# A 26-product block algorithm for ten of eleven bodies of each FFN up projection

## The reference

```
def conv_ffn(x, w_in, conv_w, conv_b, w_out):
    h = causal_dwconv(x @ w_in, conv_w, conv_b)
    gate, val = h[..., :D_FF], h[..., D_FF:]
    return (jax.nn.gelu(gate) * val) @ w_out
...
def _conv_ffn(h, w_up, conv_w, conv_b, w_down):
    u = _dwconv(h @ w_up, conv_w, conv_b)
    gate, val = jnp.split(u, 2, axis=-1)
    return (jax.nn.gelu(gate, approximate=True) * val) @ w_down
```

## Time and profile before

| | us |
|---|---|
| median of 3 runs | 3307.51 |
| lowest and highest run | 3304.76 and 3310.20 |
| span of the profiled execution | 3308.8 |
| TensorE busy in it | 3243.1 |
| VectorE, ScalarE, GpSimd busy | 1734.4, 1034.2, 1227.8 |

### The profile page before, as it was taken

The page is one execution under the profiler, slowest core; times in us unless marked ns, Lnnn a source line. Parts: engine busy times, 40 slices in busy tenths (PEclk is TensorE's granted clock), DMA queues, the critical chain, the costliest instruction groups (busy, mean ns, idle before and its releaser), DMA issues.

```text
span 3308.8 us, 51491 instructions
## 1 busy us (share of the span) xinstructions
PE 3243.1 (98%) x16994; PEld 2617.8 (79%) x16994; DVE 1734.4 (52%) x2856; ACT 1034.2 (31%) x2119; POOL 1227.8 (37%) x983
## 2 busy tenths in 40 slices
PE   9999999999999999999999999999999999999998
PEld 7787888867777788886446888878888688788887
DVE  6675446555555545646446555345463544354544
ACT  3533233123333323313326333133221334223312
POOL 4344444323221345442001343444443431544444
PEclk9999999999999999999999999999999999999999
DMA  3223222221111222222211211222222211122222
GB/s 136 77 84 102 78 93 82 77 82 59 58 52 39 77 95 77 82 95 71 70 45 32 58 57 57 83 70 83 95 82 96 71 52 65 52 83 95 83 91 81
DMA packets 68682, 249.53 MB, mean 75 GB/s; under 512 B 7568, under 2 KB 7568, under 8 KB 68544
## 3 DMA queue, kind: packets, MB, share of 16 engines
q1 hardware_dynamic: 68544, 247.72, 22.7%
HBM read 245.59 MB, written 2.10 MB: 75 GB/s over the span
## 4 chain that ended last, share of the span: by engine, by line
PE 91%; DVE 4%; ACT 2%; issue 2%; DMA 0%; DVEq 0%; SPq 0%; ACTq 0%
PE psum L2434 56%; PE psum L545 6%; PE psum L2369 5%; PE psum L2611 4%; PE psum L1964 3%; PE psum L1497 3%; PE psum L1524 2%; PE psum L1989 1%; PE psum L577 1%; PE psum L2623 1%; PE psum L1551 1%; PE psum L615 1%; ACT scratch L1211 1%; PE psum L599 1%; DVE stream L3003 1%
## 5 line engine op out<-in xcount | busy, mean ns | idle before, releaser
L2434 PE MATMUL psum<-scratch 128*128 128x256 f32 (+2 forms) x3600 | 809.5, 381 | 0.3 <-issue 0.2
L2434 PEld LDWEIGHTS psum<-scratch 128*128 128x128 f32 x3600 | 683.6, 190 | 101.4 <-issue 1.9
L3286 POOL TENSOR_TENSOR scratch<-w_ring 128x512 f32<-128x512 f32 (+2 forms) x160 | 201.0, 1256 | 1114.2 <-DMA w_ring<-units 901.4
L2699 ACT ACTIVATE scratch<-psum 128x256 f32<-128x256 f32 (+2 forms) x480 | 184.8, 386 | 852.5 <-PE psum L2434 821.9
L3106 DVE TENSOR_TENSOR scratch<-scratch,psum 128x256 f32<-128x256 f32 (+2 forms) x264 | 107.8, 422 | 485.5 <-PE psum L2434 471.6
L2434 PE MATMUL psum<-scratch,w_ring 128*128 128x256 f32 (+2 forms) x1200 | 274.0, 381 | 0.0
L2434 PEld LDWEIGHTS psum<-scratch,w_ring 128*128 128x128 f32 x1200 | 227.9, 190 | 33.3
L2434 PE MATMUL psum<-acts,w_ring 128*128 128x256 f32 (+2 forms) x1088 | 245.1, 383 | 1.2 <-ACT acts L2115 0.9
L2434 PEld LDWEIGHTS psum<-acts,w_ring 128*128 128x128 f32 x1088 | 207.0, 191 | 32.7 <-ACT acts L2115 1.2
L3293 POOL TENSOR_TENSOR scratch<-w_ring 128x512 f32<-128x512 f32 (+2 forms) x160 | 229.8, 1436 | 0.0
L2784 ACT ACTIVATE scratch<-scratch,params 128x512 f32<-128x512 f32 (+2 forms) x176 | 144.0, 818 | 272.1 <-DVE scratch L3106 272.1
(11 more groups left out here) (495 smaller groups left out, 4981.7 us busy)
## 6 DMA issues: line engine op xcount, KB each, us to landing
w_ring<-units SPq DMA_DIRECT2D x463, 512.0 KB, 3.7
residual<-x_t SPq DMA_DIRECT2D x4, 528.0 KB, 6.0
out_t<-residual SPq DMA_DIRECT2D x2, 512.0 KB, 3.4
out_t<-residual SPq DMA_DIRECT2D x1, 768.0 KB, 4.4
params<-cols SPq DMA_DIRECT2D x1, 568.5 KB, 10.4
out_t<-residual SPq DMA_DIRECT2D x1, 256.0 KB, 3.3
gate_w_sb<-gate_w SPq DMA_DIRECT2D x1, 96.0 KB, 10.1
```

Source lines behind the costliest of these rows:

```text
L2434: mm = nc.tensor.matmul(out, weights(k), moving(k), start=(p in (1, 2, 5) and k == 0), stop=(k == h - 1), skip_group_check=(p != 2))
L2699: nc.scalar.activation(kept(q, n, H), quad_bank(q, p, H, b), ACT.Copy).then_inc(q_copied, 1)
L3286: g.tensor_tensor(s(1), row(1, 0), row(1, 1), ALU.add).then_inc(q_weight, 1)
```

## The change

The first body of each FFN up projection stays two quads. The ten others treat their 4 units as a whole: weights in 4 x 4 blocks (unit by quarter of the input features), input in 4 x 2 blocks (quarter of the features by half of the tokens). A product is now two matmuls, and a table of 26 products takes the place of the 28 pairs of matmuls of two quads: 52 matmuls a body. The tables also say what each engine does: `RANK_PRODUCTS` names for each product its weight block (under 16 one of the ring, else buffer number plus 16), how many of POOL's sums must be done, its input block, its bank and whether it opens the bank. `RANK_SUMS` lists POOL's 18 instructions of a body, 29 sums of 128x256, eleven instructions making two sums each (128x512 in all), into 16 buffers in `SCR`. `RANK_TERMS` lists to which rows a product is added: 8 first terms are copied by ACT, 18 later ones added or subtracted by DVE. `RANK_MOVING` lists 20 sums of the input, made once an FFN by DVE. The semaphores `r_product`, `r_weight`, `r_first` and `r_later` are the old `x_loaded0` to `x_loaded3`, and `r_moving` is the old `lru_conv`.

`W` gets four more slots, `WX`, at the end of `SCR`, and an FFN's units alternate between the two sets of four. The convolution now runs by half rows (T/2 tokens) in two banks of PSUM: ACT writes the first tap to the bank, DVE adds the two others in place, ACT takes the gelu from there to `A`, and DVE multiplies `A` by the other bank. These steps of body j-1 stand between the terms of body j, at the places in `PIECE_AT`. `xp` exists twice. The mixer's tables move into `SCR`. The sums of the input for the down projection are spread over the last bodies.

```diff
+RANK_PRODUCTS = (
+    (19, 2, ('v', 0, 0), 'turns', True),
+    (22, 4, ('x', 1, 1), 3, True),
+    (13, 0, ('v', 1, 0), 4, True),
+    (24, 5, ('x', 2, 0), 'turns', False),
+    (26, 6, ('v', 2, 0), 3, False),
+    (27, 7, ('v', 5, 0), 4, False),
...
+    (6, 0, ('v', 17, 0), 4, True),
+    (17, 18, ('v', 16, 0), 'turns', False),
+    (15, 0, ('x', 3, 0), 2, True),
+)
+RANK_SUMS = (
+    ('add', ((0, 2, 10), (1, 5, 13),), 0, 0),
+    ('add', ((2, 1, 16), (3, 6, 17),), 1, 0),
+    ('sub', ((4, 8, 9), (5, 10, 11),), 0, 0),
+    ('add', ((6, 19, 20),), 3, 0),
...
+    ('add', ((1, 13, 1),), 0, 0),
+)
+PIECE_AT = (1, 7, 13, 19)
...
+            def rank(n, j, src, H):
...
+                        pe.wait_ge(r_weight, rank_weighed(n, j, sums))
...
+                    for q in range(2):
+                        mm = nc.tensor.matmul(PS[:, bank, 0:H], weights(q), moving(q), start=(opens and q == 0), stop=(q == 1),
+                                              skip_group_check=True)
+                    mm.then_inc(r_product, 1)
...
+            def rank_weights(n, j):
...
+                    for buffer in RANK_SUM_AGAIN[at]:
+                        if j > 1:
+                            pool.wait_ge(r_product, rank_done(n, j - 1, RANK_LAST_USE[buffer] - 1))
...
+                    g.tensor_tensor(blocks([RANK_BUFFERS + o for o, _, _ in sums]), blocks([a for _, a, _ in sums]), blocks([e for _, _, e in sums]),
+                                    ALU.add if op == "add" else ALU.subtract).then_inc(r_weight, 1)
...
+                    nc.scalar.activation(PS[:, 6 + val, 0:H], scratch(2128 * (j % 2), 4, 532)[:, 2 * pair + val, half * H:half * H + H],
+                                         ACT.Identity, bias=PAR[:, w0 + 3:w0 + 4], scale=PAR[:, w0:w0 + 1]).then_inc(shared("tap", name), 1)
...
+                    y = PS[:, 6 + val, 0:H]
+                    v.scalar_tensor_tensor(out=y, in0=xps[j % 2][:, 2 * pair + val, half * H + k:half * H + k + H], scalar=PAR[:, w0 + k:w0 + k + 1],
+                                           in1=y, op0=ALU.mult, op1=ALU.add).then_inc(shared("mid" if k == 1 else "conv", name), 1)
...
-                with pe.Fori(0, NF // 2) as i:
-                    quads(i, BODIES[name], UNITS[name], KD // 2, T, CHUNKS[name], lambda k, t, e: h(k)[:, t:e], ready=normed)
+                quads(0, BODIES[name], UNITS[name], KD // 2, T, CHUNKS[name], src, ready=normed)
+                for j in range(1, RANK_UP + 1):
+                    rank(n, j, src, T // 2)
```

More of the change, by code:

```diff
@@ L102 @@
         CHUNK_LAST.append(_b - 1)
+CHUNK_HALF = [(c + 1) % 2 for c in range(len(CHUNK_LAST))]
+for _name in ("ffn0", "ffn1", "ffn2", "ffn3"):
+    _c = CHUNKS[_name]
+    CHUNK_HALF[_c + 1], CHUNK_HALF[_c + 2], CHUNK_HALF[_c + 3] = CHUNK_HALF[_c], 1 - CHUNK_HALF[_c], CHUNK_HALF[_c]
 class Chain:
@@ L3125, in ffn @@
[L3125 to L3134 removed]
+                        moving(chunk, m, KD // 2, src, H, T)
```

615 lines of the change are left out of this document (488 added, 127 removed).

## The result

The changed kernel takes **3477.39 us** (median of four runs, 3476.34 to 3478.85). The kernel before took 3307.83 us in the runs beside it. The ratio is 1.0513, with a 95% interval of 1.0498 to 1.0527, so the change costs 5.1%. The forecast was 3410 us with a range of 3365 to 3460. The direction was right and the size was 67 us too small: the measured time lies 17 us above the upper end of the range. The profiled execution has a span of 3477.1 us.

The account below looks back on a forecast made before the run. The prediction took TensorE, busy 98% of the span, as the bound now, with POOL's late start adding waits after the change. From 3307.5 us, +68 + 4 + 31 = +103 gave 3410 us, 80% range 3365 to 3460.

Parts of the forecast that it names:

- fewer matmuls and down projection, nothing waits: Up bodies go from 56 to 52 matmuls, saving 70 us if TensorE never waits; down projection adds 4 us.
- gaps behind POOL, bodies 2 to 10: TensorE waits for POOL before the first, second and sixth products: 3.53 to 3.69 us a body.
- clock in those bodies: Clock falls in half of the 36 new bodies, 1.7 us each: +31 us, ends 0 and 61.
- the first of the ten bodies: VectorE enters the body after the two-quad one late, 1 to 3 us, taken as 2; body called even.
- +68: Bodies 2 to 10 in four FFNs: net loss of 1.76 to 1.96 us a body, clock falls not included.
- POOL's place: POOL starts a body's sums only after the previous body's 25th product, since they write buffer 1: 3.53 us wait in ffn0.
- third gap: Before a body's sixth product, TensorE waits 0.25 us for POOL's seventh instruction.
- The expected rows: Profile would show TensorE idle for POOL, some 36 times 2.1 and 1.15 us, and TensorE, not DMA, releasing POOL.
- The rival on the other side: TensorE never waits and the up bodies lose 70 us: 3242 us; chance that it hardly waits 0.06.
- POOL's 1.27 us: POOL's 512-wide sums in the new bodies keep 1.27 us beside VectorE, not 1.73 us.
- clock stays up: Rival: no clock falls in the new bodies, all else as forecast: 3380 us, range 3365 to 3390, chance 0.27.
- Banks behind VectorE and ScalarE: In new bodies both free PSUM banks in time; 0 to 1 us a body if not. POOL-or-banks-late or clock-always-down case: 0.20.

Follow-up runs that it names:

- finer spread: Changed kernel with buffer 12 for the 25th product, VectorE's four awaited sums earlier, eight late input sums after products 2 to 13, not 2 to 9: 3248.63 us.
- filled gaps: Changed kernel plus unused matmuls in bodies 2 to 10, four before a body's first product and two before its second: 3436.69 us.
- other buffer: Changed kernel with the last of POOL's 18 sums written to buffer 12, not 1, and read there by the 25th product: 3292.98 us.
- VectorE's order: Changed kernel with four awaited two-quad sums ahead of late input sums; those eight spread over the next body, 3445.36 us, or made at once, 3461.81 us.

## Why the forecast was right in direction and short in size

The table sets the forecast's terms beside what the runs give for each, in us.

| term | forecast | measured | from |
|---|---|---|---|
| fewer matmuls and down projection, nothing waits | -66 | -59 | finer spread against the kernel before beside it |
| gaps behind POOL, bodies 2 to 10 | +131 | +142 | filled gaps against the other buffer, body by body |
| clock in those bodies | +31 | +47 | changed kernel against filled gaps, body by body |
| the first of the ten bodies | +7 | +44 | other buffer against finer spread |
| sum | +103 | +174 | measured as a whole: +170 |

(In the forecast a body saves 1.78, 1.74, 1.73 and 1.73 us. Its "+68" is 131 less nine such savings, and its "even" gives the saving of the first body back, 7 us.) The measured column goes from kernel to kernel and ends where it began, so that it closes on 170 is no proof of its terms; the proof is that the same losses came off one by one and in pairs. The +44 leaves out the 8 us by which the first body is still longer in the finer spread. They are in the -59, where 7 us are missing from the saving. No run shows the forecast's +4 for the down projection by itself.

**POOL's place, right.** The instruction that writes buffers 0 and 1 starts 0.17 us after the 25th product, where 0.08 was taken. The gaps come from the second, fourth and seventh of POOL's instructions and sum nearly to what was worked out: 142 - 131 = 11 us more, or 0.3 us a body, and the fillers' own cost is still in this number. With the gaps filled the second product starts 2.05 us after the first and the sixth 6.11 us after it (387.20, 389.25 and 393.31); the forecast had 2.04 and 5.85. So it is the third gap that came out longer. This term alone outweighs the saving. The expected rows came: 34.4 us in 40 waits put down to POOL, which are the 36 second products and the sixth products of the four bodies without a fall of the clock, and POOL released by TensorE. The first gap has to be looked for under "issue", not under POOL as the forecast said. The rival on the other side, that TensorE never waits, fell: no 512-wide sum takes under 1.2 us, and TensorE's order is what it was read to be.

**POOL's 1.27 us, right.** In bodies 2 to 10 its 512-wide sums stay at this beside VectorE's new instructions, which read one operand from PSUM. Slowed ones, as the 1.73 us of the earlier trace rows, are not what makes the gaps, which have the length worked out from 1.27. The Trainium skill, "SBUF — State Buffer", section "Who interferes with whom", says that a VectorE instruction with at most one SBUF input doesn't contend with GpSimd, and that one with two does where GpSimd's reads SBUF too. By that rule the gaps are as forecast, and the trace agrees. The second half of the rule was cited for POOL and not turned on VectorE, and there it mattered. These are two groups by line, with least, median and most in nanoseconds. The first is POOL's sums, the second VectorE's input sums, which read two operands from SBUF:

```profile
L3766 POOL TENSOR_TENSOR scratch<-scratch x420: 713/1267/1772, 305.6 to 3317.0; 128x512 f32<-128x512 f32 x80, 128x256 f32<-128x256 f32 x60
```

```profile
L3457 DVE TENSOR_TENSOR scratch<-residual x10: 681/1752/1787, 308.5 to 1201.3; 128x528 f32<-128x528 f32 x5, 128x516 f32<-128x516 f32 x5
```

The input sums take 0.70 us while POOL is idle (320.46 and 321.08 above) and some 1.75 us beside its sums (330.62 to 334.03). Of the eighty in the four FFNs, the 32 that overlap no sum of POOL take 0.68 to 0.71 us, and 40 of the other 48 take 1.10 to 1.80. No experiment took POOL away from them, so this is read from the timeline, not shown by a run. The trace of the kernel before had the sign. The forecast read the POOL sum at 709.15 as one beside VectorE instructions with an operand in PSUM. One such runs there, and then, still beside POOL, one with both operands in SBUF. It takes 1.04 us where the same line took 0.43 at 705.64:

```profile
709.68 1.04 DVE L3003 TENSOR_TENSOR stream<-scratch,stream 128x264 f32 x1
```

**The first body, the step that failed.** The forecast put the delay at "1 to 3 us on this, take 2, and call the body even". It cost 44 us in four FFNs, 11 us each, by the kernels that take it away. The forecast counted only the last four input sums and what they delay in the first new body. It didn't ask who waits for VectorE while it makes the sixteen sums ahead of these: the sums L3465 in the same queue, and behind the first two of these the last products of the two-quad body. It knew both lengths of such a sum (0.76 and 1.55 us) and took 2 us, less than four of the short ones. With 1.38 to 1.79 us each the four late sums take 6.4 us, not 3.0. The two waits, 4.47 and 3.89 us, are some 34 us in four FFNs, and the rest came from the slow products behind them (6.44 us for 16 records). The experiments with VectorE's order took 32 us of it back in the changed kernel, and 44 with the finer spread in the kernel with the other buffer.

**The clock, right mechanism, too small.** "Falling in half of the 36 bodies costs 18 x 1.7": the clock in fact fell in or behind the gaps of 32 of the 36 bodies, in nine of them for twice as long. This body of ffn1 has one of the long ones:

```profile
1365.00:1370.00 5.00, 2.39 (x9) 1.19 (x7) 0.87 (x3) 0.53 (x2) 4.57 (x5) 0.87 0.85 312
1370.00:1375.00 5.00, 4.91 (x12) 3.90 (x13) 1.40 (x3) 1.58 (x4) 4.92 (x5) 0.50 0.01 4
1375.00:1380.00 5.00, 5.00 (x23) 4.33 (x22) 2.51 (x7) 2.39 (x6) 4.76 (x5) 0.95 0.00 0
```

(0.13 + 0.50 + 0.05) x 5 us is 3.4 us of full speed lost, twice the 1.7 taken from the earlier trace rows. In all 23 x 1.7 + 9 x 3.4 = 70 us of full speed were lost, more than the forecast's upper end of 61. The price in time was 47 us, not 31, because "nothing covers a slow product" was wrong too: the gaps, the third among them, covered a part. Two errors offset each other here. The rival "clock stays up" fell. The Trainium skill, "TensorE: Matmul & The Clock Gate", section "Why this matters for your kernels", warns only of idle gaps longer than any here. By that rule this term would have been 0. The longest gap at the head of bodies 2 to 10 is 2.08 us, and the clock fell, so the measurement decides against reading the rule as a safe limit.

**Banks behind VectorE and ScalarE, right for bodies 2 to 10.** VectorE's taps (L3474), which write back to PSUM, take longer than the 0.43 us of the nearest row. The result's place is hardly the reason: another `scalar_tensor_tensor` with one operand in PSUM (L2478) writes to SBUF and takes 475 ns for 128x256, and the taps take 482 at that shape. Groups by line, L2478 by shape: busy time and mean ns, then idle time before.

```profile
L3474 DVE SCALAR_TENSOR_TENSOR psum<-scratch,params,psum 128x256 f32<-128x256 f32 (+2 forms) x704 | 312.2, 485 | 133.0 <-ACT psum L3082 133.0
L3506 DVE TENSOR_TENSOR scratch<-scratch,psum 128x256 f32<-128x256 f32 (+2 forms) x720 | 299.5, 422 | 327.0 <-PE psum L2665 220.2 <-ACT scratch L3102 101.8
...
L3082 ACT ACTIVATE psum<-scratch,params 128x256 f32<-128x256 f32 (+2 forms) x352 | 189.7, 564 | 43.0 <-DVE acts L3483 26.7 <-DVE scratch L3506 10.0 <-ACT acts L3091 0.4
...
L2478 DVE SCALAR_TENSOR_TENSOR scratch<-scratch,psum 128x256 f32<-128x256 f32 x48 | 20.0, 475 | 9.0 <-PE psum L2291 9.0
```

The cover held all the same: with the other buffer TensorE runs at 23.14 us a body and waits for neither. (The forecast's 38 x 0.33 is 12.5 us, not 12.7, which changes nothing.)

**The range.** It ended at 3460, "where POOL's slower sums and some falls of the clock meet". Of the four terms all came out above the forecast, and the first body by most. With 11 us an FFN for the first body the same sum gives 3447, and with 47 for the clock 3463. The other 14 us are within the 11 us of the gaps and the 7 us missing from the saving.

## What to carry to other kernels

When a list of sums and products is packed into few buffers, look which of the next round's sums comes first and which is the last product that reads its target: one buffer number decided 184 us here. When new work is put on an engine's queue, ask of every instruction behind it who waits for it, at the length that the new work has beside its noisiest neighbour, and do so for the ramp as well as for the steady loop. A gap in front of TensorE costs more than its length: 142 us of gaps drew 47 us of clock behind them.

## What the runs showed of the hardware

- The clock fell though no gap in bodies 2 to 10 was longer than 2.08 us: two gaps of some 2.0 and 0.97 us in each body of some 28 us brought the granted clock from 1.00 to 0.91 (ffn0) and 0.93 (ffn1). Matmuls of no use in the gaps kept it at 1.00 and made the kernel 41 us faster.
- A fall can cost less time than it takes of full speed: in ffn0 18 us of full speed were lost between bodies 2 and 10, and about 14 us of time. What falls on an idle TensorE, or on products that would have waited next, isn't paid.
- VectorE's sums with both operands in SBUF took 0.70 us alone and up to 1.80 us beside POOL's, while a POOL sum of 1.27 us took up to 1.77 us. By these times each lengthens the other.
- On VectorE a `scalar_tensor_tensor` with one operand in PSUM took 482 ns with its result in PSUM (L3474) and 475 with it in SBUF (L2478), both 128x256; a `tensor_tensor` of that shape into SBUF (L3506) took 420. ScalarE's first taps (L3082, SBUF to PSUM, with a scale and a bias by partition) took 564 ns and its copies out of PSUM (L3102) 388; they differ in more than the target, so no run says what makes the difference.
